# A quarter of a score block ahead of each batch of one-hot products, and a wait on ScalarE moved into the expert loop

## The reference, cut to what matters

```python
def peer_ffn(h, w_q, keys, u_tab, v_tab):
    ...                                   # scores of 8 heads against two sets of 128 keys
    expert = e1 * N_KEYS + e2             # 16 experts of each head for each token
    gate = jax.nn.softmax(best, axis=-1)
    ...
    u_sel = jnp.take(u_tab, et, axis=0)
    act = jax.nn.gelu(jnp.einsum('tkd,td->tk', u_sel, xt), approximate=False)
    v_sel = jnp.take(v_tab, et, axis=0)
    return jnp.einsum('tk,tkd->td', gt * act, v_sel)
```

## Time and profile before

| what | value |
|---|---|
| median of 3 runs | 1708.95 us (1708.61 to 1709.91) |
| the profiled execution | 1708.64 us, span of the instructions 1706.8 us |
| busy: TensorE, its weight loads | 1694.1 us, 1498.7 us |
| busy: VectorE, ScalarE, GpSimd | 1393.3, 742.8, 675.9 us |
| weight stage | from 717.5 to 903.6 us |
| expert loop | from 915 to 1698 us |

### The profile page before, as it was taken

One profiled execution on the slowest core, in us unless ns is written; L12 is line 12 of the kernel. 1 busy time (PEld: TensorE's weight loads), 2 busy tenths in 40 slices (PEclk: granted clock), 3 DMA queues, 4 the chain that ended last, 5 costly groups with the idle time before them and its releaser, 6 DMA issues.

```text
span 1706.8 us, 33761 instructions
## 1 busy us (share of the span) xinstructions
PE 1694.1 (99%) x12005; PEld 1498.7 (88%) x12005; DVE 1393.3 (82%) x2763; ACT 742.8 (44%) x1059; POOL 675.9 (40%) x555
## 2 busy tenths in 40 slices
PE   9999999999999999999999999999999999999998
PEld 6878888788888999999998888888888888888887
DVE  5379989565788999999996988887778888777886
ACT  5555445543423333477773433333333333333333
POOL 0000000010253666688873554443435444344440
PEclk9999999999999999999999999999999999999999
DMA  5221132253321555566669999999999999999982
GB/s 186 86 75 40 55 96 77 83 204 123 112 84 70 175 175 170 188 240 231 242 228 358 391 394 392 325 335 345 342 374 343 342 333 338 336 352 354 352 310 98
DMA packets 158288, 399.07 MB, mean 234 GB/s; under 512 B 12512, under 2 KB 78176, under 8 KB 156416
## 3 DMA queue, kind: packets, MB, share of 16 engines
q1 hardware_dynamic: 118496, 252.20, 42.2%
q0 software_dynamic: 39712, 145.77, 22.8%
HBM read 353.75 MB, written 44.04 MB: 233 GB/s over the span
## 4 chain that ended last, share of the span: by engine, by line
PE 84%; DVE 11%; DMA 2%; ACT 1%; issue 1%; SPq 1%; DVEq 0%; ACTq 0%
PE unit L425 84%; DVE oneh L2124 1%; DMA vraw<-v_tab 1%; DVE oneh L2114 1%; DVE ci L2100 1%; DVE ci L2095 1%; DVE oneh L2118 1%; DVE best L2098 1%; DVE cscr L2096 1%; DVE best L2093 1%; DVE cand L2089 1%; DMA g_dram<-ge 0%; SPq L1083 0%; DMA xin<-xT 0%; DVE accs L2201 0%
## 5 line engine op out<-in xcount | busy, mean ns | idle before, releaser
L425 PE MATMUL unit<-h2H,uH 128*128 128x384 f32 x1024 | 349.1, 341 | 0.2 <-ACTq L1493 0.2
L425 PE MATMUL unit<-h2L,uH 128*128 128x384 f32 x1024 | 343.8, 336 | 0.0
L2327 POOL DMA_INDIRECT ring<-u_tab,idx x128 | 204.1, 1594 | 221.1 <-DVE accs L2201 194.8
L425 PE MATMUL unit<-vH,aH 128*128 128x512 f32 x768 | 237.9, 391 | 0.7 <-DVE aL L2176 0.5
L425 PE MATMUL unit<-vH,aL 128*128 128x512 f32 x768 | 237.3, 390 | 0.0
L425 PE MATMUL unit<-vL,aH 128*128 128x512 f32 x768 | 237.2, 390 | 0.0
L2327 POOL DMA_INDIRECT ring<-v_tab,idx x128 | 149.8, 1171 | 198.5 <-DVE ring L2187 188.5
L425 PE MATMUL unit<-h2H,uL 128*128 128x384 f32 x1024 | 204.0, 336 | 0.0
L1167 ACT ACTIVATE ge<-unit 128x384 f32<-128x384 f32 x128 | 62.4, 487 | 321.2 <-PE unit L425 321.2
L425 PEld LDWEIGHTS unit<-h2H,uH 128*128 128x128 f32 x1024 | 192.5, 188 | 2.8 <-issue 0.4
L425 PEld LDWEIGHTS unit<-h2L,uH 128*128 128x128 f32 x1024 | 192.6, 188 | 2.4
(11 more groups left out here) (313 smaller groups left out, 3192.8 us busy)
## 6 DMA issues: line engine op xcount, KB each, us to landing
uraw<-uT SPq DMA_DIRECT2D x128, 512.0 KB, 7.3
vraw<-v_tab SPq DMA_DIRECT2D x128, 512.0 KB, 8.6
wraw<-wall SPq DMA_DIRECT2D x68, 512.0 KB, 3.7
w_dram<-wst SPq DMA_DIRECT2D x12, 2048.0 KB, 6.7
wg<-w_dram SPq DMA_DIRECT2D x31, 768.0 KB, 9.5
g_dram<-ge SPq DMA_DIRECT2D x64, 192.0 KB, 1.9
gl<-g_dram SPq DMA_DIRECT2D x32, 384.0 KB, 10.9
gate_dram<-gst POOLq DMA_DIRECT2D x16, 256.0 KB, 2.3
```

Source lines behind the costliest of these rows:

```text
L425: return pe.matmul(out, lhsT, rhs, start=start, stop=stop, skip_group_check=True)
L2327: pool.indirect_dma_start(out=ring[k][:, :], out_offset=None, in_=(u_tab, v_tab)[half], in_offset=bass.IndirectOffsetOnAxis(ap=idx[:, SR * ...
```

## The change

Three edits. On TensorE, quarter 1 of block 39 is issued before the wait for the last picks, ahead of the transposes of the picks, and no longer behind them. In the weight stage each quarter is issued ahead of its batch of one-hot products, and no longer behind it; the matmuls are the same. On ScalarE, the wait for the stored gelus ahead of the expert loop is taken out, and each gelu of the loop waits for the count of its own buffer instead.

```diff
@@ TensorE, end of the picking
             scores(PRE_T - 1, 1, 0)
+            scores(PRE_T - 1, 1, 1)
             pe.wait_ge(ee_picked, TT)
             across("e2T", 1, lambda t: ee[:, t, 1, :])
             across("e1T", 0, lambda t: ee[:, t, 0, :])
-            for quarter in range(1, 4):
+            for quarter in range(2, 4):
                 scores(PRE_T - 1, 1, quarter)
@@ TensorE, weight stage
                         batch = 16 * i + 4 * j + b
+                        scores(PRE_T + 4 * i + j, j % 2, b)
                         pe.wait_ge(oh2_ready, batch + 1)
...
                         last.then_inc(wmm_done, 1)
-                        scores(PRE_T + 4 * i + j, j % 2, b)
@@ ScalarE, expert loop
             def own_gelu(q, s):
                 act.wait_ge(act_ready, G * q + s + 3)
+                act.wait_ge(g_stored[s], 16 * NPRE // 2)
                 gelu(NPRE + 2 * q + s, s)
...
-            for s in range(2):
-                act.wait_ge(g_stored[s], 16 * NPRE // 2)
```

## The result

Over 13 runs each, the changed kernel takes 1712.95 us and the kernel before 1709.91 us (medians): a ratio of 1.0019, 95% interval 1.0012 to 1.0026. The forecast was 1709.0 us and the range ended at 1711.4. The change costs 3 us, and the range did not hold it. Of the 3.95 us between forecast and measurement 0.96 us are the base: the median of three runs, 1708.95 us, from which the forecast counts, became 1709.91 us over 13.

What follows compares the result with a forecast made beforehand. TensorE, busy 1694.1 of 1706.8 us, was taken as the bound, so only its holes could be won. Terms 0 - 0.54 - 0.16 + 0.70 + 0.1 = +0.1 us on 1708.95 gave 1709.0 us, range 1707.3 to 1711.4.

Steps and rivals of the forecast that it cites:

- A quarter into the wait for the picks: TensorE before the pick transposes: 1.06 us of matmuls fit the hole, transposes start at 713.10 as before.
- Quarters ahead of the batches: TensorE's weight stage: batches keep their times, the 1.06 us won becomes a wait on ScalarE's copy; sum 0 us.
- ScalarE's wait: Ahead of the expert loop: ScalarE goes on near 906.3, TensorE's 0.54 us wait at the first unit is gone.
- What is late next: Second lap's value loads, then VectorE's chain: TensorE waits 0.70 us near 957, plus 0.1 us for a later landing.
- The upper bound: Second lap's load: last two gathers land ahead of it, 1.05 MB at 410 GB/s is 2.6 us, reduced to 1.3.
- The rule of the Trainium skill: DMA engines alternate between queues per packet; the load would keep its share, shift 0 or below, sum 0.1 to 0.7 lower.
- a shift of 1 us and more: Second lap's load landing this much later would speak against DMA engines taking turns between queues a packet at a time.
- The second rival: Gathers coming forward crowd the second lap's load, TensorE's wait near 957 grows: 1710.3 to 1711.6 us; chance 0.13.
- the upper price: Most that crowding of the second lap's load was to add to TensorE's wait near 957: 2.6 us.

Runs made afterwards that it cites:

- e6: Changed kernel plus gathers of value rows held for the second lap's loads and 16 x1 transposes ahead of the wait for ScalarE's last copy; 1710.66 us, ratio 1.0003.
- e10: Kernel before plus TensorE's quarter edits and 16 x1 transposes ahead of the wait for ScalarE's last copy; 1709.92 us against 1710.15, ratio 0.9999.
- e2: Kernel before plus ScalarE's edit alone, quarters still behind their batches; 1712.77 us against 1710.53, ratio 1.0015.
- e3: Changed kernel plus GpSimd's first gathers of value rows held until the second lap's weights and stored activations landed; 1708.14 us against 1710.53, ratio 0.9992.

## Why the prediction was wrong, point by point

- **A quarter into the wait for the picks**: right. The quarter ends its last start at 713.34, the transposes follow at 713.82.
- **Quarters ahead of the batches**: right. Batch 0 stands at T + 4.30 (before T + 4.44) behind 0.28 us of idle time, which the profile puts down to no engine ("issue") and no longer to VectorE, so that its operands are what it waits for is not shown. The pitch is 1.934 us, and the gain becomes a wait of 1.12 us on ScalarE's copy. The transposes came 0.3 us earlier where 0.2 was allowed. e6 and e10 show that the gain was indeed lost in this wait: with the transposes split, the wait is gone and they start 1.0 and 1.9 us earlier.
- **ScalarE's wait**: right as far as the first unit. ScalarE starts at 905.12, right behind its last gelu, where 906.3 was expected, behind the transposes; the 0.54 us are gone, the stores hold nothing up in the loop.
- **What is late next**: the chain was the right one, VectorE's from the second lap's tiles to its last low half. The failed step is the term behind it, "I take 0.1 us later, between 0.7 us earlier and 1.3 us later, because the gathers' queue is kept filled past 936 either way". Counted from T, the gates came 1.9 and 2.6 us later in the two profiled executions of the changed kernel; with T itself, 0.7 and 0.5 us later, that is the 2.7 and 3.1 us by which the end moved. The reason given was wrong: from 920 to 928 the kernel before had 463 packets of gathers against 1529 of loads, and GpSimd waited 10.8 us for VectorE's dot products; the loads used these gaps. ScalarE's earlier start closed them. The gathers' shift was mis-sized too: the first came 0.5 us later and not 2.4 us earlier, the last 3.7 us earlier and not 5.
- **The upper bound** was wrong with it. It counted whole gathers that land behind 938.5 and divided them by the rate of all engines. The crowding sits earlier, while the loads go in small packets: where packets of the two go about one for one, a load's 0.54 KB (0.43 MB / 792 in e2) takes turns with 3.6 KB of a gather.
- **The rule of the Trainium skill** (DMA: Bandwidth & Descriptors, section Queues, rings and completion order), turns a packet at a time, was not what failed. The rows agree with it, in packets as the profile counts them: 457 packets against 460 from 928 to 936 in the changed kernel, 729 against 792 in e2. Whether these are the packets that the rule means, no run shows. The prediction took a shift of 1 us and more as a sign against the rule, and the shift came; but what failed is what the prediction drew from the rule, that the load keeps its share. The load keeps its turns; it loses bytes when the other queue, which had gaps before, is kept filled with larger packets.
- **The second rival** (crowding, 0.13) is what came about, by the mechanism named. TensorE's wait stood at the second lap's first unit (1.85 us), not near 957; the time went beyond the upper price, 3.0 us by the medians where 2.6 were the most, while the shift of the gates alone, 1.9 and 2.6 us, lies within it. It had "the crowding queue is as full before" against it, the same error. The clock that fell in one execution of the changed kernel was not foreseen, and cost nothing there.

## What to carry to other kernels

A wait that seems to hold one engine up for nothing may be what paces another engine's transfers: before taking it away, list what the released engine releases in turn, down to the queues of the DMA engines, and look whether their packets are large beside those of the loads that are due next. A gain in one hole has to be followed to the next engine that TensorE meets; in nine of the twelve executions here the end was the later of two sums, first unit + 784.25 and gates + 758.38, and an edit that moves the earlier one is worth nothing. When a queue is said to be full, read its packets by stretches; a DMA share near 1 doesn't tell whose bytes they are.

## What the runs showed of the hardware

The two DMA queues of the changed kernel from 928 to 936, when the loads are value tiles in 4 KB rows:

```profile
q0 software_dynamic: 457, 1.67, 52.3%
q1 hardware_dynamic: 460, 1.61, 50.7%
```

In these stretches the DMA engines moved about as many packets of the one queue as of the other (457 and 460 here, 729 and 792 in e2 from 920 to 928): about the same bytes here, and six times the bytes for the gathers in e2, whose loads then come in packets of 0.54 KB. That both queues had work throughout is read from these counts, not shown by a row of its own. The granted clock fell to 0.50 for about 3 us after TensorE had waited 1.9 us in one execution of the changed kernel, 2.8 us in e2 and 2.3 us in e3, and stayed at 1.00 after 2.5 us in another execution of the changed kernel and in e6. In the changed kernel and e2, where VectorE's chain set the end, the fall cost nothing; in e3, where TensorE's own work behind the wait did, it cost 1.6 us.
